# Who normalises the softmax weights: moving the scaling of both attentions from ScalarE to VectorE

## The reference, cut to what matters

```python
# sliding window: 16 query heads of 64, window 128, with a sink in the softmax
p = softmax(concatenate([s, sink], -1), -1)[..., :-1]
out = einsum('bnhgqk,bnkhd->bnqhgd', p, vv)
# forgetting attention (FoX): 8 heads of 128, causal over all 1024 keys
p = softmax(where(mask, s, NEG_INF), -1)
out = einsum('bhqk,bkhd->bqhd', p, v)
```

## Time and profile before

| what | us |
|---|---|
| median of 3 runs (2972.0 to 2977.24) | 2975.76 |
| the profiled execution's own time | 2979.88 |
| its span | 2978.2 |
| PE busy | 2724.7 (91%) |
| DVE busy | 1763.4 (59%) |
| ACT busy | 1235.3 (41%) |
| POOL busy | 279.3 (9%) |

### The profile page before, as it was taken

The page is one execution under the profiler, slowest core; times in us unless marked ns, Lnnn a source line. Parts: engine busy times, 40 slices in busy tenths (PEclk is TensorE's granted clock), DMA queues, the critical chain, the costliest instruction groups (busy, mean ns, idle before and its releaser), DMA issues. The chain is left out here.

```text
span 2978.2 us, 39168 instructions
## 1 busy us (share of the span) xinstructions
PE 2724.7 (91%) x12257; PEld 2195.7 (74%) x12257; DVE 1763.4 (59%) x2734; ACT 1235.3 (41%) x2281; POOL 279.3 (9%) x300
## 2 busy tenths in 40 slices
PE   4799989999998999999989999999959999999895
PEld 2477767777786777777768888888847888888684
DVE  5745556686565666766675555555655455644335
ACT  4422224333334555555565445545443332334111
POOL 0000000111120000000001111111130001024002
PEclk8799999999999999999999999999979999999997
DMA  8355663566664333333354544454464444555342
GB/s 271 121 183 192 187 200 121 128 149 151 161 156 97 108 101 111 108 111 111 101 185 107 112 108 89 101 113 85 106 174 134 148 169 167 172 169 176 135 143 102
DMA packets 326299, 414.22 MB, mean 139 GB/s; under 512 B 18833, under 2 KB 229841, under 8 KB 322513
## 3 DMA queue, kind: packets, MB, share of 16 engines
q1 hardware_dynamic: 283584, 338.84, 36.0%
q0 software_dynamic: 29584, 66.09, 12.2%
q10 hardware_dynamic: 13056, 8.39, 1.0%
HBM read 293.71 MB, written 119.55 MB: 139 GB/s over the span
## 5 line engine op out<-in xcount | busy, mean ns | idle before, releaser
L1142 DVE TENSOR_TENSOR w_lo<-w_sum,w_hi 128x512 fp32r<-128x512 f32 x336 | 230.1, 690 | 215.0 <-ACT w_hi L759 211.7
L1625 PE MATMUL pC<-b_hi,w_hi 128*128 128x512 f32 x784 | 313.7, 400 | 37.8 <-ACT ctile L773 27.8
L1625 PE MATMUL pA<-b_hi,w_hi 128*128 128x512 f32 x784 | 315.1, 402 | 35.9 <-DVE w_lo L1142 13.8
L1625 PE MATMUL pD<-b_hi,w_hi 128*128 128x512 f32 x784 | 311.7, 398 | 19.7 <-ACT ctile L773 13.5
L1625 PE MATMUL pA<-b_lo,w_hi 128*128 128x512 f32 x784 | 311.2, 397 | 0.0
L166 ACT CAST w_hi<-w_raw 128x1024 fp32r<-128x1024 f32 x128 | 135.1, 1055 | 424.0 <-PE zP L2290 208.7
L1625 PE MATMUL pA<-b_hi,w_lo 128*128 128x512 f32 x784 | 310.9, 397 | 0.0
L1625 PE MATMUL pC<-b_hi,w_lo 128*128 128x512 f32 x784 | 310.7, 396 | 0.0
L1625 PE MATMUL pC<-b_lo,w_hi 128*128 128x512 f32 x784 | 309.2, 394 | 0.0
L1625 PE MATMUL pD<-b_hi,w_lo 128*128 128x512 f32 x784 | 308.1, 393 | 0.0
L1625 PE MATMUL pD<-b_lo,w_hi 128*128 128x512 f32 x784 | 308.1, 393 | 0.0
(11 more groups left out here) (254 smaller groups left out, 5207.5 us busy)
## 6 DMA issues: line engine op xcount, KB each, us to landing
w_raw<-in_w_in_dram SPq DMA_DIRECT2D x84, 1024.0 KB, 8.1
proj_scratch<-ctile SPq DMA_DIRECT2D x168, 256.0 KB, 2.2
proj_scratch<-ctile POOLq DMA_DIRECT2D x168, 256.0 KB, 5.8
bg_raw<-in_w_ada_dram SPq DMA_DIRECT2D x64, 512.0 KB, 6.0
w_raw<-in_w_out_dram SPq DMA_DIRECT2D x64, 512.0 KB, 3.9
w_raw<-in_w_br_swa_dram SPq DMA_DIRECT2D x32, 512.0 KB, 4.1
w_raw<-in_w_br_fox_dram SPq DMA_DIRECT2D x32, 512.0 KB, 3.9
aux<-proj_scratch SPq DMA_DIRECT2D x64, 256.0 KB, 4.0
```

The costliest lines, as they stand in the source:

```text
L1142: nc.vector.tensor_tensor(ring(k, True), factor(k), ring(k, False).bitcast(F32), ALU.subtract).then_inc(in_lo, 1)
L1625: last = nc.tensor.matmul(bank(r, k)[:], w[:, j, :], b[:, j, :], start=(k < 4 and n == 0), stop=(n == 11), skip_group_check=True)
```

## The change

ACT no longer multiplies the weights. DVE, right behind its reciprocal, waits for that reciprocal and multiplies: in the sliding window with one tensor_tensor over all four heads (128x1024, the second operand broadcast along the row from a 128x4 tile), in FoX with one tensor_scalar over the block's (i+1)*128 keys. It raises `norm_ready` itself. ACT's waits for `inv_ready` go with its multiplications.

```diff
@@ scalar, sliding window
-                    def normalise(e):
-                        act.wait_ge(inv_ready, 2 * u + (e + 1))
-                        for i in range(4):
-                            ins = nc.scalar.activation(sp_w[:, i], sp_w[:, i], ACT.Copy, scale=row_inv[:, i:i + 1])
-                        ins.then_inc(norm_ready, 1)
...
                     exponentials(0)
-                    passed(at[1], at[1] + 1)
-                    normalise(0)
-                    passed(at[1] + 1, at[2])
+                    passed(at[1], at[2])
...
                     passed(at[3], at[4])
-                    normalise(1)
                     half_out(0)
@@ scalar, FoX
-                    def normalise(i):
-                        w = fp_w[:, 0:i + 1, :].rearrange("p j t -> p (j t)")
-                        act.wait_ge(inv_ready, 32 + 8 * h + (i + 1))
-                        nc.scalar.activation(w, w, ACT.Copy, scale=row_inv[:, 0:1]).then_inc(norm_ready, 1)
...
                         exponentials(i)
-                        normalise(i)
@@ vector, sliding window
                         nc.vector.reciprocal(row_inv[:], row_inv[:]).then_inc(inv_ready, 1)
+                        dve.wait_ge(inv_ready, s + 1)
+                        w = sp_w[:].rearrange("p i k t -> p i (k t)")
+                        nc.vector.tensor_tensor(w, w, row_inv[:].unsqueeze(2).broadcast_to([P, 4, 2 * P]), ALU.mult
+                                                ).then_inc(norm_ready, 1)
@@ vector, FoX
                         nc.vector.reciprocal(row_inv[:, 0:1], row_sum[:, 0:1]).then_inc(inv_ready, 1)
+                        dve.wait_ge(inv_ready, 32 + 8 * h + (i + 1))
+                        w = fp_w[:, 0:i + 1, :].rearrange("p j t -> p (j t)")
+                        nc.vector.tensor_scalar(w, w, row_inv[:, 0:1], None, ALU.mult).then_inc(norm_ready, 1)
```

## The result

| kernel | median us | lowest to highest | ratio to before (95% interval) |
|---|---|---|---|
| before (4 runs beside the changed one) | 2976.44 | 2972.0 to 2977.24 | |
| changed (4 runs) | 2931.24 | 2922.06 to 2933.62 | 0.9845 (0.9822 to 0.9869) |
| changed, on another occasion (5 runs; before there 2972.43) | 2923.81 | 2915.21 to 2929.27 | 0.9835 (0.9815 to 0.9855) |

The change makes the kernel 45 to 49 us faster, each time against the kernel before of the same occasion; 34.9 had been forecast.

A forecast was written before the change was run, and what follows sets the result against it. PE was taken to set the pace, so only its idle time behind ACT's queue could be won: 23.7 us in the first attention plus 11.2 in FoX, 34.9 off 2975.76, giving 2941 us; range 2929 to 2962.

The forecast's parts named there:

- E: First attention, first unit of a pair: PE's 1.17 us stall for w_lo of product n = 9; goes, 9.4 us.
- A: First attention: PE's 1.00 us stall per pair at the bank for n = 12; shrinks by about 0.7, 5.6 us in all.
- C: First attention, second unit of a pair: PE's 0.80 us stall at the bank for n = 19; goes seven times, 5.7 us.
- B: First attention: PE's 2.39 us stall per pair at the bank for n = 13, behind exponentials(0); stays, 20 us in all.
- fpT: FoX: PE's wait once a head, 9.2 us in all; 0.85 of each 1.15 goes, 6.8 us, leaving about 2.5.
- spT_lo: First attention, half e = 0: PE's stalls at spT_lo vanish but for the last unit's, 2.6 - 1.76 = 0.9 us.
- The direct wait: Start of the first attention: PE's 1.4 us wait for the normalised weights shrinks by 0.6; FoX's by 1.0 in all.
- Ends: First attention's last unit: the 2.63 us stall goes, but PE then waits for spT_lo behind DVE's splitting; 1.5 us gained.
- 4 (more than the stalls, 47 us): Rival: shorter stalls also spare most drops of the granted clock and B shrinks; 35 + 12 = 47 us, 2929; chance 0.10.
- 2 (the load's chain stays): Rival, first attention: w_raw's load doesn't move, A grows by what E gives; 19 us left, 2957; chance 0.17.
- 3 (FoX gives nothing): Rival, FoX: DVE puts in what ACT leaves out, so only 23.7 us are gained, 2952; chance 0.12.
- 1 (DVE late): Rival, first attention, half e = 1: a product of 3.7 us makes w_lo late; 9 us slower, 2985; chance 0.07.

The follow-up runs named there:

- half e = 1 alone: Changed kernel, but in the first attention DVE multiplies only for e = 1 and ACT for e = 0 as before: 2939.6 us, 0.9902 of before.
- the second experiment: Kernel before with only FoX's 64 multiplications moved from ACT to DVE, the first attention's left on ACT: 2961.61 us, 0.9935 of before.

## Why the prediction was right, and where it was short

The sign, the place and the mechanism were right: E, A and C went with ACT's queue and B stayed. PE's idle time was forecast closely. The gain was forecast 10 to 14 us too small, mostly because a term was missing. That the sums of idle time come so near is in part luck: the end and fpT gave less than forecast, A and a wait marked issue gave more.

- *Idle time of the first attention.* Predicted within the stage: 9.4 + 0.9 + 5.7 + 5.6 + 0.6 = 22.2. Measured: 44.4 to 22.7 and 21.2, so 21.7 and 23.2.
- *E, 9.4:* gone, by the steps given (DVE's 2.39 us wait has gone, w_lo comes 1.20 sooner, against 1.15). That either half is nearly enough for it was not seen.
- *C, 5.7:* gone, with half e = 1 alone, as the step says.
- *A, 5.6 of it:* larger than given. Measured from the reciprocal, the load goes out 1.2 us sooner, ACT rounds it 1.4 sooner, and PE starts product n = 9 0.3 sooner (4.91 to 4.62 us). Counted from that start, ACT's emptying of pD's bank begins at 9.66 us where it was 10.81, so the chain gained 1.15 on PE, not 0.7, and A went nearly whole: pD's waits fell from 9.5 to 2.5. Both halves are needed for that, so what half e = 0 gives was not the small matter that the prediction made of it.
- *spT_lo, 0.9:* gone but for the last unit's. *The direct wait, 0.6:* 1.4 became 1.7 and 0.9 in two profiles: nothing.
- *Ends, 1.5:* wrong. The 2.63 went, but the wait for spT_lo behind DVE's splitting of b panels grew from 1.76 to 4.6: 2.63 + 1.76 - 4.6 = -0.2. What PE gained came back whole as this wait.
- *B:* stays, as said. The experiment on it shows an error of ACT's order alone.
- *FoX, 11.2:* PE's idle time over seven heads fell by 9.3, against 7/8 of 11.2 = 9.8. The bank's 3.4 went, the direct wait lost 0.9, as said. fpT fell from 9.2 to 5.4, not to 2.5; the prediction had allowed 0.3 us a head for an emptying that waits for its matmul, and why more is left no run shows. One wait marked issue fell by 1.5 instead (5.2 to 3.7), for which there was no term.
- *The products:* 1.225 us (1.22 taken), and in FoX 0.286 to 0.755, median 0.52, each about 0.05 above the line drawn.

**The missing term.** The sum took a stall at the idle time before its matmul. A stall costs more, as the records around stall C of the kernel before show:

```profile
1128.08 0.39 PE L1625 MATMUL pD<-b_lo,w_hi 128*128 128x512 f32 x1
1128.31 0.39 PE L1625 MATMUL pD<-b_hi,w_lo 128*128 128x512 f32 x1
1129.50 0.47 PE L1625 MATMUL pA<-b_hi,w_hi 128*128 128x512 f32 x1 [0.80 <-ACT ctile L773]
1129.80 0.39 PE L1625 MATMUL pA<-b_lo,w_hi 128*128 128x512 f32 x1
```

While PE runs on, a matmul starts 0.23 us behind the one before, and its record of 0.39 overlaps the next by 0.16. The last one before a wait overlaps nothing, so 0.16 of the loss is entered as busy time. The first one behind the wait is followed after 0.30, another 0.07. Behind some stalls the granted clock falls too, here after B of the pair before (a window of PE, its busy time, PEclk, DMA):

```profile
1033.30:1036.30 3.00, 3.00 (x9) 0.50 0.10 39
1034.16 0.63 PE L1625 MATMUL pC<-b_hi,w_lo 128*128 128x512 f32 x1
1034.59 0.63 PE L1625 MATMUL pC<-b_hi,w_hi 128*128 128x512 f32 x1
```

The matmuls are 0.43 us apart there, 0.20 more each; these are the "slow" ones of the table. A straight line through the fourteen profiles gives busy = 512.7 + 0.23 x slow + 0.29 x stalls, the largest miss being 2.0 us. For the 23 stalls that went that is 6.7 us. The slow matmuls fell from 45 to 10 in one profile of the changed kernel and to 33 in the other, which is 8.1 or 2.8 us. With the idle time this makes 21.7 + 6.7 + 8.1 = 36.5 and 23.2 + 6.7 + 2.8 = 32.7; measured were 35.7 and 32.8. In FoX's seven heads the stalls fell from 21 to 9 and the slow matmuls from 16 to 8 (11 in the second profile): 3.5 + 1.8 = 5.3 of the 6.6 us that PE was less busy. So the forecast lacked 10 us for the stalls (6.7 + 3.5) and 4 to 10 for the clock. With 1.7 off at the end, 3.0 off at fpT and some 2 more for A it would have been 34.9 + 10.2 - 1.7 - 3.0 + 2 = 42, and 46 to 52 with the clock. With PE's idle time in the place of the number of stalls the line fits worse (misses up to 2.8 us), which speaks for the number and not the length.

**The rivals.** 4 (more than the stalls, 47 us) has the size that was measured, by a mechanism that is right in part. B did not shrink, and the 0.29 us a stall was not in it. But it counted on fewer dips of the clock, and there were fewer: 41 to 50 slow matmuls in the three profiles with the old stalls, 10 to 47 in the five with few, 26 in the mean. That is about 4 us of the gain in the mean, where the rival had 12 together with B, and it varies: 10 and 47 slow matmuls go with stages of 541.8 and 549.1 us at equal idle time, in two kernels with the same instructions there. The column of the loads hides this. A load takes 0.19 us at the full rate and 0.33 in a dip (at 1032.55 and 1034.16 in the kernel before), yet their sum is 431.4 to 433.4 in the three and 429.9 to 435.7 in the five. 2 (the load's chain stays) and 3 (FoX gives nothing) fell with the load's rows and the second experiment. 1 (DVE late) was not this kernel's case, but nearly its case was made: a product that is ready at 3.51 us gives 2983.95, where the rival said 2985 for 3.7. That is luck in part: the rival, too, priced stalls at their idle time, and the dearest new wait, for the weights themselves (15.4), it did not name. Its threshold of about 2.4 us, below which w_lo would not be later, does not hold for the time: at 2.39 us 22 of the 45 us are gone already. By a straight line between the two points the change turns into a loss at about 3.2 us (an estimate).

**The rule that spoke against it.** With DVE 67% and then 78% busy, moving work from ACT to DVE gained 1.5%. The loss begins close by, at 80% (456.5 of 571.0 us) and 82% (490.0 of 600.2), where one and two more reductions stand. The Trainium skill, page "Perfetto Trace Analysis", section "Optimizing Scalar/DVE Operations", says that offloading from a saturated DVE may make sense. These runs agree that a DVE without room decides, and show that the share over a stage does not tell it; the gaps in the timeline behind the step do.

## What to carry to other kernels

Look at what stands in an engine's queue behind an operation, not at which engine is busier: ACT was at 56% and its 1.71 us of work in the wrong place cost 32 us, while a wait of the same engine in the same place cost nothing. Count each stall of PE at its idle time plus what its matmul records no longer overlap (here 0.2 to 0.3 us), look for dips of the clock behind it, and before moving work at all see whether one emptying of a bank could stand in front of the step that waits: that one step gave 22 to 29 us. Put the same reduction or activation into a kernel as a dummy to measure the room that an engine has left.

## What was not expected of the hardware

- A tensor_tensor whose second operand is broadcast along the row costs the plain price: 1224 to 1228 ns for 128x1024, against 1216 with a plain operand. The Trainium skill, page "VectorE: DVE Perf Modes", section on the TRN2 errata, gives (N + 151)/0.96 ns for the plain fp32 add, held exact at 512 and 2048 elements. An estimate from it is 1224 ns at 1024; the trace agrees, for a multiplication with this operand.
- FoX's tensor_scalar with a per-partition operand takes 286 ns at 128 and 755 at 1024 elements, so 0.52 ns an element and 0.22 us fixed. The line through the forms in the earlier trace rows has 0.50 and 0.18.

```profile
L1502 DVE TENSOR_SCALAR fp_w<-fp_w,row_inv x64: 286/520/755, 1503.7 to 2115.9; 128x128 f32<-128x128 f32 x8, 128x256 f32<-128x256 f32 x8, 128x384 f32<-128x384 f32 x8, 128x512 f32<-128x512 f32 x8
```
